# The modulation rows move from TensorE in the mixers to ScalarE and VectorE in the feed-forward parts

## What is computed

```
swiglu(x, w_gate, w_up, w_down) = (silu(x @ w_gate) * (x @ w_up)) @ w_down
for l in range(2):
    h = h + 0.5 * swiglu(rmsnorm(h, ffn1_norm[l]), ...)     # w_gate, w_up: 1024 x 2816
    h = h + concat(retention, differential attention) @ w_out[l]
    h = h + 0.5 * swiglu(rmsnorm(h, ffn2_norm[l]), ...)
mod = silu(c) @ w_mod + b_mod     # shift, scale, gate of both halves of the second block
```

## Time and profile before

| | us |
|---|---|
| median of 3 runs | 1758.71 (1757.97 to 1759.53) |
| the profiled execution | 1757.33 |
| its span in the trace | 1755.4 |
| TensorE busy | 1735.8 (99%) |
| VectorE busy | 896.8 (51%) |
| ScalarE busy | 691.0 (39%) |
| GpSimd busy | 157.8 (9%) |

### The profile page before, as it was taken

How to read it: one execution, slowest core, us unless ns; L and a number is a source line. 1 busy time by engine, 2 the same in 40 slices (tenths; PEclk the granted TensorE clock), 3 DMA queues, 4 the chain that set the end, 5 groups by cost and what they waited for, 6 DMA issues and landing times.

```text
span 1755.4 us, 30166 instructions
## 1 busy us (share of the span) xinstructions
PE 1735.8 (99%) x12541; PEld 1419.2 (81%) x12542; DVE 896.8 (51%) x1558; ACT 691.0 (39%) x1167; POOL 157.8 (9%) x167
## 2 busy tenths in 40 slices
PE   8999999999999999999999999999999999999998
PEld 8999988999999999998899999677774445444444
DVE  6655576676555766567678666475421121111212
ACT  6444545364444544455455445453521111111111
POOL 1000042210000100014314000100300000000000
PEclk9999999999999999999999999999999999999999
DMA  9545464545544554456556555232299999999997
GB/s 380 197 174 182 153 254 168 199 171 180 178 169 168 178 183 168 172 179 227 204 183 226 189 184 180 81 85 73 118 388 367 428 428 428 428 429 429 429 427 319
DMA packets 78815, 425.89 MB, mean 243 GB/s; under 512 B 16352, under 2 KB 32992, under 8 KB 41824
## 3 DMA queue, kind: packets, MB, share of 16 engines
q1 hardware_dynamic: 78256, 421.01, 62.6%
q10 hardware_dynamic: 432, 3.10, 0.4%
HBM read 423.03 MB, written 1.05 MB: 242 GB/s over the span
## 4 chain that ended last, share of the span: by engine, by line
PE 90%; DMA 6%; ACT 2%; DVE 2%; issue 1%; POOL 0%; POOLq 0%; SPq 0%; DVEq 0%; ACTq 0%
PE ps L714 18%; PE ps L716 18%; PE ps L715 18%; PE ps L1340 10%; PE ps L1391 5%; DMA ring<-stream_expert 5%; PE ps L1314 3%; PE ps L1042 2%; PE ps L1036 2%; PE ps L1048 2%; PE ps L1288 2%; PE ps L808 1%; ACT w_split L1453 1%; PE ps L1321 1%; DVE w_split L1882 1%; PE ps L1322 1%
## 5 line engine op out<-in xcount | busy, mean ns | idle before, releaser
L1882 DVE TENSOR_TENSOR w_split<-ring,w_split 128x1024 fp32r<-128x1024 f32 x335 | 424.7, 1275 | 334.2 <-ACT w_split L1453 333.6
L714 PE MATMUL ps<-x_hi,w_split 128*128 128x272 f32 (+1 forms) x1856 | 541.1, 292 | 3.4 <-DVE x_lo L1887 2.3
L716 PE MATMUL ps<-x_hi,w_split 128*128 128x272 f32 (+1 forms) x1856 | 534.0, 288 | 0.0
L715 PE MATMUL ps<-x_lo,w_split 128*128 128x272 f32 (+1 forms) x1856 | 532.0, 287 | 0.0
L1453 ACT ACTIVATE w_split<-ring 128x1024 fp32r<-128x1024 f32 x335 | 350.6, 1054 | 354.9 <-PE ps L716 353.7
L714 PEld LDWEIGHTS ps<-x_hi,w_split 128*128 128x128 f32 x1856 | 350.2, 189 | 15.7 <-issue 10.0
L715 PEld LDWEIGHTS ps<-x_lo,w_split 128*128 128x128 f32 x1856 | 350.3, 189 | 0.3
L716 PEld LDWEIGHTS ps<-x_hi,w_split 128*128 128x128 f32 x1856 | 350.1, 189 | 0.0
L716 PE MATMUL ps<-hid_hi,w_split 128*128 128x272 f32 (+1 forms) x704 | 201.7, 287 | 0.0
L715 PE MATMUL ps<-hid_lo,w_split 128*128 128x272 f32 (+1 forms) x704 | 201.6, 286 | 0.0
L714 PE MATMUL ps<-hid_hi,w_split 128*128 128x272 f32 (+1 forms) x704 | 201.2, 286 | 0.0
(11 more groups left out here) (418 smaller groups left out, 2136.6 us busy)
## 6 DMA issues: line engine op xcount, KB each, us to landing
ring<-stream_ffn SPq DMA_DIRECT2D x131, 1024.0 KB, 4.8
ring<-stream_expert SPq DMA_DIRECT2D x48, 2048.0 KB, 24.8
ring<-stream_expert SPq DMA_DIRECT2D x36, 1024.0 KB, 11.3
arena<-stream_expert SPq DMA_DIRECT2D x16, 2048.0 KB, 25.3
ring<-stream_in SPq DMA_DIRECT2D x27, 1024.0 KB, 4.9
ring<-stream_mod SPq DMA_DIRECT2D x24, 1024.0 KB, 7.0
con<-stream_expert SPq DMA_DIRECT2D x8, 2048.0 KB, 25.9
ring<-stream_out SPq DMA_DIRECT2D x12, 1024.0 KB, 5.0
```

The source lines that it names most:

```text
L714: pe.matmul(to, w[:, 0, k], hi, start=first, stop=False)
L715: pe.matmul(to, w[:, 0, k], lo, start=False, stop=False)
L716: return pe.matmul(to, w[:, 1, k], hi, start=False, stop=last_)
L1882: nc.vector.tensor_tensor(w[:, 1], half_of(n), w[:, 0].bitcast(fp32), ALU.subtract).then_inc(split_ready, 1)
```

## The change

The product of `silu(c)` and the matrix is no longer taken on TensorE. A unit (q, v) is one fill q multiplied by one vector v: both vectors for q = 0 to 7, the first alone for q = 8 to 23, 32 units in all. ScalarE multiplies the eight chunks of 128 inputs x 256 columns, each by its column of `silu(c)` as a per-partition scale: four chunks at the end of step j, four at the end of step j + 1. VectorE adds the eight chunks to one at the end of its step j + 2, in three instructions with drains between, and writes the sum of a unit (128 partitions x 256) into one of three buffers `mod_sums`. A portion is two units. TensorE sums its partitions with four matmuls, whose weights are a column of ones at one place among 32 (`unit_row`), in the spare columns of the bank of `up`, ahead of a step's own matmuls. It waits first for the second add of the portion. VectorE adds the result to `mod_row` when it evicts that bank.

The first eight fills serve two units each; the first product goes to a buffer of its own, the second is written over the fill. From q = 8 the one product is written over the fill. SP waits for the last add of a fill before it reuses the slot. The fills go to where their units are: part 0 has units 0 to 7, part 1 units 8 to 19, part 2 units 20 to 31, each with eight in the gate/up steps, and four in the down steps of parts 1 and 2. The mixers' fills are the weights alone. The two batches become columns by one transpose each, at x = 25 of the two mixers; none is left for the second block. On POOL the `memset` of `dv` now goes ahead of `sum_squares`, with one semaphore less.

```diff
-MOD_SLOTS, MOD_MIX = 24, 11
+MOD_SLOTS = 24
...
+MOD_UNITS = [(q, v) for q in range(8) for v in range(2)] + [(q, 0) for q in range(8, MOD_SLOTS)]
+MOD_FFN = [range(0, 8), range(8, 20), range(20, 32), range(0)]
+MOD_EARLY = [(3, 5, 7, 9, 11, 13, 15, 17), (1, 3, 5, 7, 10, 12, 15, 17), (1, 3, 5, 7, 10, 12, 15, 17), ()]
+MOD_LATE = [(), (1, 6, 11, 16), (1, 6, 11, 16), ()]
+MOD_BUFFERS = 3
+PORTIONS = [{9: 0, 13: 1, 17: 2, 21: 3}, {7: 4, 11: 5, 16: 6, 21: 7}, {1: 8, 2: 9, 7: 10, 11: 11, 16: 12, 21: 13}, {}]
+MIXER_PORTIONS, PORTIONS_AT = [(), (14, 15)], 8
+MOD_FIRST = [0, 4]
+
+
+def mod_units(f, early):
+    n = len(MOD_EARLY[f])
+    return dict(zip(MOD_EARLY[f], MOD_FFN[f][:n])) if early else dict(zip(MOD_LATE[f], MOD_FFN[f][n:]))
+
+
+def ffn_fills(f):
+    behind = {j + 1: MOD_UNITS[u] for j, u in mod_units(f, True).items()}
+    behind.update({GU_SLOTS + (i + 3) // 2: MOD_UNITS[u] for i, u in mod_units(f, False).items()})
+    fills = []
+    for s in range(FFN_SLOTS):
+        fills.append(("ffn", f, s))
+        if s in behind and behind[s][1] == 0:
+            fills.append(("mod", behind[s][0]))
+    return fills
...
 FILLS = []
 for _l in range(DEPTH):
-    FILLS += [("ffn", 2 * _l, s) for s in range(FFN_SLOTS)]
-    for q in range(IN_SLOTS):
-        FILLS += [("in", _l, q)] + ([("mod", _l * MOD_MIX + q - 1)] if 1 <= q < 1 + MOD_MIX else [])
+    FILLS += ffn_fills(2 * _l)
+    FILLS += [("in", _l, q) for q in range(IN_SLOTS)]
     FILLS += [("out", _l, s) for s in range(OUT_FILLS)]
-    FILLS += [("ffn", 2 * _l + 1, s) for s in range(FFN_SLOTS)]
-FILLS += [("mod", DEPTH * MOD_MIX + q) for q in range(MOD_TAIL)]
+    FILLS += ffn_fills(2 * _l + 1)
 FILLS += [("in2", name) for name in IN2] + [("out2", r) for r in range(OUT_SLOTS // 2)]
...
+LAST_UNIT = {("mod", q): u for u, (q, _) in enumerate(MOD_UNITS)}
...
+        mod_product = cut(arena, rest + (F + 4 + 2 * HID_SPLITS) * T, C, MOD_COLS)
+        mod_sums = cut(ring, X_AT, MOD_BUFFERS, 2, MOD_COLS)
...
-                        sp.wait_ge(raw_done, RAW_AT[before] + 1)
+                        sp.wait_ge(mod_summed, LAST_UNIT[before] + 1)
...
+                    if j in PORTIONS[f]:
+                        mod_portion(PORTIONS[f][j], 2 * (j % 4) + 1)
...
-            def mod_rows(q):
-
-                w = raw_slot(("mod", q), C, MOD_COLS)
-                if q == 0:
-                    pe.wait_ge(cc_ready, 1)
-                batch, k = divmod(q, MOD_MIX)
-                pe.wait_ge(mod_ready, batch + 1)
-                end = min(MOD_MIX, MOD_SLOTS - batch * MOD_MIX) - 1
-                own = cc[:, :, 32 - 2 * k:64 - 2 * k]
-                for c in range(C):
-                    last = pe.matmul(ps[32 * (c % 4):32 * (c % 4) + 32, 5, 256:512], own[:, c], w[:, c], start=k == 0 and c < 4,
-                                     stop=k == end and c >= C - 4)
-                last.then_inc(raw_done, 1)
+            def mod_portion(p, bank, col=T):
+
+                batch = int(p >= MOD_FIRST[1])
+                n = p - MOD_FIRST[batch]
+                pe.wait_ge(mod_summed, 2 * p + 2)
+                if n == 0:
+                    pe.wait_ge(mod_ready, batch + 1)
+                for i in range(2):
+                    for j in range(2):
+                        own, at = 2 * n + j, 64 * i + 32 * j
+                        last = pe.matmul(ps[at:at + 32, bank, col:col + P], unit_row[:, 32 - own:64 - own], mod_sums[:, p % MOD_BUFFERS, j, i * P:i * P + P],
+                                         start=True, stop=True)
+                last.then_inc(mod_used, 1)
 
             def mod_turn(batch):
 
                 pe.wait_ge(mod_row_ready, batch + 1)
-                for i in range(2):
-                    last = pe.matmul(ps[:, 5, 256 + 32 * i:256 + 32 * i + 32], mod_row[:, i * P:i * P + P], K("pick"), start=True, stop=True)
-                last.then_inc(mod_turned, 1)
+                pe.transpose(ps[:, 5, 256:384], mod_row, ident).then_inc(mod_turned, 1)
...
+                    if x == PORTIONS_AT:
+                        for k, p in enumerate(MIXER_PORTIONS[l]):
+                            mod_portion(p, 5, k * P)
...
-                    if x % 2 == 1 and 0 <= (x - 3) // 2 < MOD_MIX:
-                        mod_rows(l * MOD_MIX + (x - 3) // 2)
...
-            mod_rows(DEPTH * MOD_MIX)
-            mod_rows(DEPTH * MOD_MIX + 1)
...
-            mod_turn(DEPTH)
...
+                def mod_products(u, half):
+
+                    q, v = MOD_UNITS[u]
+                    m = FILL["mod", q]
+                    w = cut(ring, m % NS * SLOT, C, MOD_COLS)
+                    to = mod_product if q < 8 and v == 0 else w
+                    if half == 0:
+                        act.wait_ge(slot_full[m % NS], full_count(m))
+                        if to is mod_product and u >= 2:
+                            act.wait_ge(mod_summed, u - 1)
+                    for c in range(4 * half, 4 * half + 4):
+                        last = nc.scalar.activation(to[:, c], w[:, c], ACT.Identity, scale=cc[:, c, v:v + 1])
+                    if half == 1:
+                        last.then_inc(mod_scaled, 1)
+
+                units = mod_units(f, True)
...
+                    for half in range(2):
+                        if j - half in units:
+                            mod_products(units[j - half], half)
+                units = mod_units(f, False)
...
-            def mod_evac(batch):
-                act.wait_ge(raw_done, RAW_AT["mod", min(MOD_SLOTS, (batch + 1) * MOD_MIX) - 1] + 1)
-                nc.scalar.activation(mod_row, ps[:, 5, 256:512], ACT.Copy).then_inc(mod_row_ready, 1)
...
-                        act.wait_ge(dv_cleared, l + 1)
+                        act.wait_ge(sq_summed, 3 * l + 2)
...
+                def mod_add(u):
+
+                    q, v = MOD_UNITS[u]
+                    p = u // 2
+                    part = mod_product if q < 8 and v == 0 else cut(ring, FILL["mod", q] % NS * SLOT, C, MOD_COLS)
+                    dve.wait_ge(mod_scaled, u + 1)
+                    nc.vector.tensor_tensor(part[:, 0:4], part[:, 0:4], part[:, 4:8], ALU.add)
+                    dve.drain()
+                    nc.vector.tensor_tensor(part[:, 0:2], part[:, 0:2], part[:, 2:4], ALU.add)
+                    dve.drain()
+                    if u % 2 == 0 and p >= MOD_BUFFERS:
+                        dve.wait_ge(mod_used, p - MOD_BUFFERS + 1)
+                    nc.vector.tensor_tensor(mod_sums[:, p % MOD_BUFFERS, u % 2], part[:, 0], part[:, 1], ALU.add).then_inc(mod_summed, 1)
...
+                    used = nc.vector.tensor_tensor(hid[:, j, t:T], ps[:, bank + 1, 0:T - t], rstd[:, t:T], ALU.mult)
+                    if j in PORTIONS[f]:
+                        used = mod_collect(PORTIONS[f][j], bank + 1)
+                    used.then_inc(gate_up_used, 1)
...
+                    if j - 2 in units:
+                        mod_add(units[j - 2])
...
+                    if i - 2 in units:
+                        mod_add(units[i - 2])
...
+            def mod_collect(p, bank, col=T):
+
+                if p in MOD_FIRST:
+                    return nc.vector.tensor_copy(mod_row, ps[:, bank, col:col + P])
+                return nc.vector.tensor_tensor(mod_row, mod_row, ps[:, bank, col:col + P], ALU.add)
...
+                    if x == PORTIONS_AT + 2:
+                        for k, p in enumerate(MIXER_PORTIONS[l]):
+                            dve.wait_ge(mod_used, p + 1)
+                            dve.drain()
+                            mod_collect(p, 5, k * P)
+                    if x == MOD_TURN_AT - 2:
+                        dve.drain()
+                        dve.sem_inc(mod_row_ready, 1)
...
+                pool.wait_ge(split_used, HALF_AT["in", l, 0] + 1)
+                nc.gpsimd.memset(dv[:, 0], 0.0)
                 sum_squares(3 * l + 1, mix_sq)
-                pool.wait_ge(split_used, HALF_AT["in", l, 0] + 1)
-                nc.gpsimd.memset(dv[:, 0], 0.0).then_inc(dv_cleared, 1)
```

More of the change, by code:

```diff
@@ L141 @@
     ("axial_cos", SEQ), ("axial_sin", SEQ), ("levels", (len(LEVELS) + 1) * P),
[L142 removed]
+    ("causal", P // 2), ("ident16", P // 2), ("ident", P), ("half_ones", P), ("earlier", P), ("iota", CAP)])
 FIRST_CON = CON["ret_cos"][0]
@@ L395, in build @@
         MOD_AT = 64
-        m = layout(small, MOD_AT, [("mod", 48, 2), ("a1", C, 2), ("a2", C), ("cc", C, 64), ("ss", 8), ("vstd", 8), ("vr", 8),])
-        mod_row = cut(arena, ARENA - MOD_COLS, MOD_COLS)
-        mod, a1, a2, cc, v_ss, v_std, v_rstd = (m[x] for x in ("mod", "a1", "a2", "cc", "ss", "vstd", "vr"))
+        m = layout(small, MOD_AT, [("mod", 48, 2), ("a1", C, 2), ("a2", C), ("cc", C, 2), ("unit", 64), ("ss", 8), ("vstd", 8), ("vr", 8),])
+        mod_row = cut(arena, ARENA - P, P)
+        mod, a1, a2, cc, unit_row, v_ss, v_std, v_rstd = (m[x] for x in ("mod", "a1", "a2", "cc", "unit", "ss", "vstd", "vr"))
```

(28 more changed lines are left out.)

20 lines of the change are left out of this document (6 added, 14 removed).

## The result

The changed kernel takes 1796.51 us (median, 1794.41 to 1798.44) against 1758.34 (1757.44 to 1759.53) of the one before, run beside it: a ratio of 1.0222 (1.0209 to 1.0234), or 38.2 us slower. The profiled execution took 1796.78, with a span of 1794.9, 39.5 longer than before. All comparisons use undisturbed executions alone; the first run of E5 has no trace of one, which is why E5 stands twice.

A forecast was written before the change was run, and what follows sets the result against it. TensorE was taken to bound the kernel, busy 99% of the span. Added 52.0, removed 29.3 and given back 7.0 us made +29.7, a forecast of 1788 us, in a range of 1748 to 1805.

The forecast's parts named there:

- The ring: Feed-forward parts: a refill behind a doubly used slot is wanted at once, ScalarE waits its 4.8 us landing; first cycle costs 6.1.
- the ring doesn't hold: Rival: the refill is not wanted that early, so cycles cost 0.8 each; net +0.4, 1759 us; chance 0.11.
- The pace of the pair: Gate/up steps: late ScalarE and VectorE take 6.1 us a step with products, 6.4 with an add, against TensorE's 6.05.
- The portion's wait for the add of step x - 2: Gate/up steps: every portion waits 0.4 us (0.1 from j = 10) for VectorE's add, plus all the lateness.
- The portions themselves: TensorE: each of 16 portions of four 128-column matmuls costs 0.6 us, 9.6 in all (8 to 12).
- The mixers: Two mixers: 22 `mod_rows` at 1.20 us removed, 26.4, with 3.5 a mixer given back as waits.
- The tail: Tail: two `mod_rows` cost 1.86 us together, and three `mod_turn` becoming two transposes saves some 1.0.
- The clock: TensorE: granted clock may fall after long waits; 0 to 5 us for the kernel, not 1.6 for each of 9.
- the last waits of three parts: Ends of three feed-forward parts: the only places left where a slow clock would cost time, within 0 to 5 us.
- The adds keep up: Rival: lateness is made good and portions find their sums ready; 13 to 20 us faster, 1739 to 1746; chance 0.17.
- The adds are dear: Rival: a VectorE add takes 3.4 us instead of 2.49; +15, 1803; shares 0.10 with the other upper cases.
- costly portions: Rival: each portion costs TensorE 1.2 us, +10 on top, 1798; shares 0.10 with the other upper cases.

The follow-up runs named there:

- E5: Changed kernel with the first two of VectorE's three add instructions and their drains left out; 1768.7 us, ratio 1.0064, in its first run.
- E9: Changed kernel with each modulation fill of the gate/up steps one weight slot later in the order of fills (j + 2, not j + 1); 1766.08 us.
- E4: Changed kernel with most of ScalarE's products left out, a half unit being one activation instead of four; 1775.08 us, ratio 1.0096.
- E7: Kernel before the change with the modulation's matmuls left out, one of 32 columns replacing eight for most fills; 1743.8 us, ratio 0.9921.
- E6: Changed kernel with eight extra matmuls of ones on TensorE ahead of its wait at the nine portions that waited longest; 1791.48 us, ratio 1.0190.
- E2: Changed kernel with each modulation fill of the gate/up steps two weight slots later in the order of fills (j + 3, not j + 1); 1766.22 us.
- E5's second run: Changed kernel with the first two of VectorE's three add instructions left out, run again for its stages; 1769.47 us, ratio 1.0069.
- E1: Changed kernel with TensorE's portions two steps later, the last ones of two feed-forward parts moved to the mixers, fills unchanged; 1783.43 us, ratio 1.0146.

## Why the prediction was right, step by step

It said 1788 in 1748 to 1805; the time is 1796.5, by the mechanism that was named. By its own steps:

- **The ring.** The refill behind the doubly used slot, wanted at once: shown. Slot released at 69.9, load 4.67, ScalarE standing still for 6.04, gate 8.1 after the release (8.2 forecast), the add ending 4.1 after its gate (4.15). The cycles of the first part are 30.2, 29.6 and 31.0 (30.3, 29.65, 29.65), of the second 32.5, 35.3 and 35.1 (30.95, 35.45, 35.45). The two that are over a us too long are those whose refill took 6.15 and 6.26 to land, where 4.85 was taken from a median; the three others on the chain took 4.67, 4.79 and 4.82. E9 gives the size: 30.4 us. The rival "the ring doesn't hold" put the kernel without it at 1759, that is 29 less than the forecast; the difference is right, its level 7 low.
- **The pace of the pair**: 6.08 and 6.47. E4 and E5 show that products and adds both count in it.
- **The portion's wait for the add of step x - 2**: the first of the three parts are 3.67, 3.96 and 2.76 (3.7, 4.0, 4.0 forecast). The portions themselves: 0.55 to 0.62 (0.6).
- **The mixers**: net right within 1.0 (-8.7) and 0.1 (-8.6), from two mistakes that cancel. The 1.20 for a `mod_rows` is what the same reading gives at most of its places (1.13 to 1.20), but the stage gave up less: 8.7 net, with 2.3 more of waits, is 11.0 of TensorE for eleven, or 1.0 each. From `scores` to `scores`, 260.72 and 271.24 in the profile before, 280.91 and 290.40 after, is 1.03 less, of which 0.09 came back as a wait. Where the missing 0.2 each goes is left open. And the mixer gave back about 2, not 3.5: its waits in the first mixer are 2.8 against 0.5, most of them for evictions and exponentials.
- **The tail**: -2.5 for 2.9. It isn't kept to the end: the shift of 37.9 at 1167 is 39.5 when the experts end, which is in the third of the profile where loads move 427 to 429 GB/s. This need not be the change: from a square of ScalarE at 1187.45 to the end are 568.0 in the kernel before, 569.6 in the changed one (from 1225.30), and 569.1 in E7 (from 1173.55), which is the kernel before but for its rows.
- **The clock** was counted at 0, with 0 to 5 allowed. This is the term that failed in size. It fell behind the nine waits of 2.1 us and more. The argument for 0 (a cycle is set by ScalarE and VectorE, a slower TensorE only waits less) holds inside the cycles, as E6 shows; by the windows the falls are some 19 us of TensorE's time (0.04 of 190 and of 225 us, 0.01 of 210, each rounded), and most of that is absorbed. The Trainium skill (TensorE: Matmul & The Clock Gate, section "Why this matters for your kernels") warned of just this after idle gaps. The trace agrees in that all nine waits of 2.1 us and more have a fall behind them, where the one of before could not say; it differs in that the Trainium skill speaks there of longer gaps than the shortest of these.
- **What the clock cost** is what the forecast named as left, the last waits of three parts, and then put at nothing. Behind the last wait of the first part, from the portion to the stage's end, are 78.69 here and 78.68 in E4, both with a fall, and 77.18 or 77.19 in E6, E9, E2 and E5's second run, all without: 1.5. From the last portion of the second part to the first of the third are 80.12, and 78.78 in E9, E2, E4 and E5's second run without a fall: 1.3. In the third part the cycle behind the first wait is 27.32, and 25.81 in E2: 1.5. That is 4.3 of the 9.8 us of span that the forecast missed. That this is near E6's 5.0 is in part chance: E6's own trace has lost the first and the third of these falls but still has the second, and some of its gain is a refill that landed in 4.74, not 6.26.
- **The missing 9.8 us of span** are then: 4.3 for the three falls; 2.7 for the two refills that took 6.15 and 6.26 (1.3 and 1.4 over 4.85), which landed in 4.66 and 4.74 at the same places in E6, and why they varied was not tried; mixers 0.9; tail and experts 2.1; start -0.4. The rest, small terms of both signs, is 0.2. Among these are the third part's first wait, 1.2 shorter than forecast, and its second, 0.8 longer.

The other rivals. "The adds keep up" is out: 12 waits, 32.8 us. "The adds are dear" and "costly portions" are out by their rows: 1.22, 0.69, 0.43, and 0.55. What `mod_evac` and the changed order on GpSimd are worth was not tried alone.

## What to carry to other kernels

When a slot of an in-order ring is used twice, find the load queued behind it and the step that wants that load: here one place in the order, in a kernel whose engines are half idle on average, was 30 us. Work moved off the bounding engine needs as many steps between its producers and the consumer as those producers are late, since a result that is asked for too early makes the bounding engine run at their pace. The two slacks are worth more together (51 us) than one by one (30 and 13), so try both before judging such a move.

## What the runs showed of the hardware

- In the changed kernel TensorE's clock fell to 1.2 GHz right behind each of nine waits of 2.1 to 5.0 us; behind waits of 0.97, 0.20 and 0.20 it stayed at 2.4. The length of the wait doesn't decide it alone: it stayed at 2.4 behind a wait of 2.74 in E2, of 2.90 in E5's second run (444 to 448 us) and of 3.28 in E1 (139 to 147 us), and fell behind one of 2.73 in E9. A fall cost 1.3 to 1.5 us where TensorE was the bound, and within 0.04 us nothing inside the cycles of the ring. Sixteen passes ahead of a wait (1.95 us) did not always prevent it: in E6 a wait of 1.85 us that followed them still had a window of 0.60 behind it, 74 to 78 us.
- Four matmuls of 128 columns with 32 columns of weights cost 0.55 to 0.62 us in a stream of 128 x 272 matmuls, and four more of them only 0.21. The larger part is paid once for the group; that it is the change of shape was not tried by itself.
- The 1 MB refills on the chain landed in 4.67, 4.79 and 4.82 us or in 6.15 and 6.26; the first of them took 4.67 in the changed kernel and 5.98 in E6, the third 6.15 and 4.66.
- ScalarE took 0.49 for one activation of 128 x 256 with a per-partition scale and 1.69 for four in a row, 0.40 each. VectorE's copy of 128 x 128 out of PSUM took 0.28.
